# Two-phase feed-forward of the last layer: earlier residual store, another product order, snapshots ahead of SiLU, token tiles copied out of PSUM

## What is computed

```
def conv_ffn(h, w_up, conv_w, conv_b, w_down):        # h: 1024 x 1024, w_up: 1024 x 5632, w_down: 2816 x 1024
    u = h @ w_up
    up = jnp.pad(u, ((0, 0), (1, 1), (0, 0)))
    u = sum(up[:, j:j + T] * conv_w[j] for j in range(3)) + conv_b
    gate, val = jnp.split(u, 2, axis=-1)
    return (jax.nn.silu(gate) * val) @ w_down
...
f = conv_ffn(modulate(x, mod[3], mod[4]), ...)
x = layer_norm(DEEPNORM_ALPHA * x + mod[5] * f, ln2_g[l], ln2_b[l])
```

## Time and profile before

| | us |
|---|---|
| runs | 3634.85, 3628.09, 3634.22; median 3634.22 |
| profiled execution | 3634.22; its span in the trace 3632.4 |
| PE busy | 3404.0 (94%) |
| DVE, ACT, POOL busy | 1758.7 (48%), 1195.3 (33%), 1181.7 (33%) |
| fast products begin and end on PE | 3007.7 and 3345.7 |
| second group of tokens begins on PE | 3481.1 |

### The profile page before, as it was taken

How to read it: one execution, slowest core, us unless ns; L and a number is a source line. 1 busy time by engine, 2 the same in 40 slices (tenths; PEclk the granted TensorE clock), 3 DMA queues, 4 the chain that set the end, 5 groups by cost and what they waited for, 6 DMA issues and landing times. The chain is left out here.

```text
span 3632.4 us, 57974 instructions
## 1 busy us (share of the span) xinstructions
PE 3404.0 (94%) x24535; PEld 2799.2 (77%) x24535; DVE 1758.7 (48%) x2801; ACT 1195.3 (33%) x1743; POOL 1181.7 (33%) x522
## 2 busy tenths in 40 slices
PE   7999999979999999999999899999979997998998
PEld 6777778867778888888887677788867676777877
DVE  4333563066266344333346633562085785556454
ACT  4334564124332111111113333573242334444322
POOL 2221101302233333333333222102214437886432
PEclk9999999999999999999999899999989999999999
DMA  5111002262211111111111111001152122223443
GB/s 195 29 23 30 1 2 65 82 195 53 58 35 35 41 35 35 41 35 41 35 41 65 26 24 48 1 2 36 57 172 82 46 99 64 87 70 118 168 140 114
DMA packets 288117, 229.46 MB, mean 63 GB/s; under 512 B 47068, under 2 KB 257908, under 8 KB 287860
## 3 DMA queue, kind: packets, MB, share of 16 engines
q1 hardware_dynamic: 286704, 225.28, 20.1%
q10 hardware_dynamic: 1156, 0.48, 0.0%
HBM read 201.60 MB, written 24.12 MB: 62 GB/s over the span
## 5 line engine op out<-in xcount | busy, mean ns | idle before, releaser
L1333 PE MATMUL psum<-h_hi,w_split 128*128 128x512 f32 (+1 forms) x4992 | 1186.6, 367 | 22.8 <-DVEq L766 6.2
L1027 POOL TENSOR_SCALAR w_split<-w_raw 128x1024 fp32r<-128x1024 f32 x142 | 403.1, 2839 | 2059.5 <-PE psum L1333 1322.6
L1333 PEld LDWEIGHTS psum<-h_hi,w_split 128*128 128x128 f32 x4992 | 847.7, 188 | 198.0 <-issue 28.4
L1333 PE MATMUL psum<-h_lo,w_split 128*128 128x512 f32 (+1 forms) x2496 | 650.9, 364 | 0.0
L1333 PEld LDWEIGHTS psum<-h_lo,w_split 128*128 128x128 f32 x2496 | 425.3, 189 | 78.5
L2762 DVE SCALAR_TENSOR_TENSOR f_t<-psum,vec,f_t 128x1023 f32<-128x1023 f32 x194 | 170.3, 916 | 397.1 <-ACT f_t L3493 395.1
L1029 POOL TENSOR_TENSOR w_split<-w_raw,w_split 128x1024 fp32r<-128x1024 f32 x142 | 349.6, 2462 | 11.8
L3493 ACT ACTIVATE f_t<-psum,vec 128x1280 f32<-128x1280 f32 (+1 forms) x53 | 73.2, 1380 | 529.4 <-PE psum L1333 516.3
L1333 PE MATMUL psum<-f_hi,w_split 128*128 128x512 f32 (+1 forms) x1056 | 239.8, 357 | 1.5 <-DVE f_t L2762 1.5
L1333 PEld LDWEIGHTS psum<-f_hi,w_split 128*128 128x128 f32 x1056 | 176.1, 188 | 36.3 <-issue 5.7
L2620 DVE SCALAR_TENSOR_TENSOR y_chan<-psum,mods,y_chan 128x1024 f32<-128x1024 f32 (+1 forms) x176 | 146.4, 877 | 97.7 <-PE psum L1333 97.5
(11 more groups left out here) (360 smaller groups left out, 5402.7 us busy)
## 6 DMA issues: line engine op xcount, KB each, us to landing
ada_late<-in_w_ada_dram SPq DMA_DIRECT2D x32, 1024.0 KB, 7.1
w_raw<-in_w_up_dram SPq DMA_DIRECT2D x56, 512.0 KB, 3.8
w_raw<-in_w_in_dram SPq DMA_DIRECT2D x42, 512.0 KB, 3.8
w_raw<-in_w_down_dram SPq DMA_DIRECT2D x40, 512.0 KB, 3.7
up_raw<-in_w_up_dram SPq DMA_DIRECT2D x32, 512.0 KB, 5.2
f_raw<-f_mid SPq DMA_DIRECT2D x44, 256.0 KB, 3.8
l_raw<-in_w_down_dram SPq DMA_DIRECT2D x17, 512.0 KB, 3.5
ada<-in_w_ada_dram SPq DMA_DIRECT2D x4, 2048.0 KB, 16.5
```

The source lines that it names most:

```text
L1027: pool.tensor_scalar(w_hi[:, n % 2], w_raw[:, n % 2], 1.0, None, ALU.mult).then_inc(s["w_hi_done"], 1)
L1333: last = pe.matmul(columns(key, t0, t0 + tn), weight, a[:, k, t0:t0 + tn], start=(k == order[0] and j == 0), stop=(closes and k == order[- ...
```

## The change

Five things are changed, all in the last layer's feed-forward.

1. The eight residual tiles are restored during f = 1 and 2 (before: 2 and 3), and SP stores them behind tile f = 1, ahead of the weights of f = 4.
2. `differences(k)` adds high and low parts first and takes 8 DVE passes in place of 10, and its 3 low parts, as well as the 4 of `h_lo`, go from DVE to POOL. The four rounds stand one place earlier, and operands 0 to 3 of the first group are split before the last `begin`.
3. The order of products: the high-channel block of Y comes second (before: fourth), the first Z product fourth (before: second); the operand of product 1 is now a plain weight block, not a sum. The snapshots and `joined` follow that order.
4. In ACT's queue `take(i - 1, 3)` and `take(i, 0)` stand ahead of `begin` of the value half and of `silu` of the tile before, which both move from the end of the group to behind them. In the last group the split of two steps' tokens and of the first weight is moved ahead of the last convs.
5. Token tiles 0 to 3 of the down projection are copied by ACT from their banks to `y_copy` (`out_of_banks`), which frees the banks; `last_norm` reads the copy. Their normalisations and stores are spread over steps n = FT + 3, FT + 5, FT + 6.

The diff, cut:

```diff
-                    if f == 2:
+                    if f == 1:
                         for k in range(KT):
                             sp.wait_ge(s["res_ready"], KT * 2 * l + k + 1)
                             sp.dma_start(r_mid[k], y_chan[:, k, 0:LAT]).then_inc(s["r_stored"], 16)
+                    if f == 2:
                         load_up(0)
...
-                    if n == FT + 3:
-                        for i in range(4):
+                    for i, behind in enumerate((4, 5, 7, 9)):
+                        if n == FT + behind:
                             store_out(i)
...
                     pool.tensor_tensor(two, one, a11, ALU.subtract).then_inc(s["sum_done"], 1)
-                    low(1, one)
+                    low(1, a12)
                     pool.wait_ge(s["sum_done"], 4 * i + 2)
...
                     pool.tensor_tensor(two, a12, two, ALU.subtract).then_inc(s["sum_done"], 1)
-                    low(3, a12)
+                    if i == 0:
+                        for k in range(4):
+                            pool.wait_ge(s["t_split_hi"], 13 + k)
+                            pool.tensor_tensor(h_lo[:, k, HALF:LAT], t_one[:, k], h_hi[:, k, HALF:LAT].bitcast(F32), ALU.subtract)\
+                                .then_inc(s["t_ready"], 1)
+                    low(3, one)
+                    pool.wait_ge(s["op_ready"], 7 * i + 4)
+                    pool.tensor_tensor(one, a11, a21, ALU.subtract).then_inc(s["sum_done"], 1)
                     pool.wait_ge(s["sum_done"], 4 * i + 4)
                     low(4, one)
...
+            def low_differences(k):
...
+                for n, (whole, t_hi, t_lo) in enumerate(((taken[:, 1], t3_hi, t3_lo), (taken[:, 0], t2_hi, t2_lo),
+                                                         (taken[:, 2], t4_hi, t4_lo))):
+                    pool.wait_ge(s["t_split_hi"], 3 * k + n + 1)
+                    pool.tensor_tensor(t_lo[:, k], whole, t_hi[:, k].bitcast(F32), ALU.subtract).then_inc(s["t_ready"], 1)
...
-                def product(i, j, bank, x_hi, x_lo, begins=True):
+                def product(i, j, bank, x_hi, x_lo, begins=True, made=None):
                     n = 7 * i + j
                     hi, lo = up_ops[n % 4][:, 0], up_ops[n % 4][:, 1]
                     wait((s["op_ready"], n + 1))
                     for k in range(KT // 2):
+                        if made:
+                            wait((s["t_ready"], made + k + 1))
...
                     product(i, 0, x_bank(i), *tokens(low, 0))
+                    wait((s["u_done"], 3 * (i - 1) + 1) if i else freed("F", l, fast_f - 1, 0))
+                    product(i, 1, Y_BANK, *tokens(high, 0))
+                    wait((s["snap_done"], 4 * i + 1))
+                    if i == 0:
+                        wait((s["t_ready"], 12))
+                    product(i, 2, x_bank(i), t2_hi, t2_lo, begins=False)
                     if i:
                         wait((s["u_done"], 3 * (i - 1) + 3))
-                    else:
-                        wait(freed("F", l, fast_f - 1, 0))
-                        wait((s["t_ready"], 16))
-                    product(i, 1, Z_BANK, *tokens(low, 1))
-                    wait((s["snap_done"], 4 * i + 1))
-                    product(i, 2, x_bank(i), t2_hi, t2_lo, begins=False)
-                    wait((s["u_done"], 3 * (i - 1) + 1) if i else None)
-                    product(i, 3, Y_BANK, *tokens(high, 0))
+                    product(i, 3, Z_BANK, *tokens(low, 1), made=None if i else 12)
+                    wait((s["snap_done"], 4 * i + 2))
+                    product(i, 4, x_bank(i), t3_hi, t3_lo, begins=False)
                     wait((s["snap_done"], 4 * i + 3))
-                    product(i, 4, x_bank(i), t3_hi, t3_lo, begins=False)
                     product(i, 5, Z_BANK, *tokens(high, 1), begins=False)
...
                 key = ("y", i)
-                y = final(i)
+                y = y_copy[:, i] if i < 4 else final(i)
...
-                dve.wait_ge(s["y_full"], i + 1)
+                if i < 4:
+                    dve.wait_ge(s["y_freed"], i + 1)
+                else:
+                    dve.wait_ge(s["y_full"], i + 1)
...
-                for n in range(2, 2 * FT):
+                for n in range(3, 2 * FT):
                     if n == FT + 3:
-                        for i in range(3):
+                        for i in range(2):
                             last_norm(i)
-                    if n == FT + 4:
-                        last_norm(3)
+                    if n in (FT + 5, FT + 6):
+                        last_norm(n - FT - 3)
...
+                    def whole(out_, row, cols):
+                        return dve.tensor_tensor(out_, h_hi[:, row, cols].bitcast(F32), h_lo[:, row, cols].bitcast(F32), ALU.add)
+
+                    if k:
+                        dve.wait_ge(s["t_ready"], 3 * k)
+                    also(whole(three, down, then))
+                    also(whole(t_scratch[:], down, first))
+                    also(whole(two, up, then))
+                    step(whole(four, up, first))
+                    step(dve.tensor_tensor(one, three, t_scratch[:], ALU.subtract))
+                    say("t_whole", dve.tensor_tensor(three, two, three, ALU.subtract))
+                    dve.wait_ge(s["t_whole"], 3 * k + 1)
+                    say("t_whole", dve.tensor_tensor(two, two, one, ALU.subtract))
                     dve.wait_ge(s["t_whole"], 3 * k + 2)
-                    tt(four, hi[:, up, first], two, ALU.subtract)
-                    tt(four, four, lo[:, up, first], ALU.add, whole=True)
...
-                        say("t_ready", dve.tensor_tensor(t_lo[:, k], whole, t_hi[:, k].bitcast(F32), ALU.subtract))
...
-                        dve.wait_ge(s["prod_done"], 7 * i + 4)
+                        dve.wait_ge(s["prod_done"], 7 * i + 2)
...
+                    for k in range(4):
+                        residual(k)
                     conv(2, 0)
-                    for k in range(3):
+                    for k in range(4, 8):
                         residual(k)
                     conv(2, 1)
                     gated(2)
-                    for k in range(3, 6):
-                        residual(k)
+                    dve.wait_ge(s["r_stored"], 2 * 16 * KT)
+                    differences(0)
                     conv(3, 0)
-                    for k in range(6, 8):
-                        residual(k)
                     conv(3, 1)
                     gated(3)
-                    dve.wait_ge(s["r_stored"], 2 * 16 * KT)
-                    differences(0)
+                    differences(1)
                     conv(4, 0)
-                    differences(1)
+                    differences(2)
...
                     gated(4)
-                    differences(2)
-                    conv(5, 0)
                     differences(3)
-                    last_differences()
...
-                            dve.wait_ge(s["snap_done"], 4 * i + (1, 2, 3)[n])
+                            dve.wait_ge(s["snap_done"], 4 * i + (1, 3, 3)[n])
                             joined(i, n)
+                            if n == 1 and i == N_FAST - 1:
+                                low_tokens(0)
+                                low_tokens(1)
+                        if i == N_FAST - 1:
+                            gate_weights(1)
                         conv(f, 0)
...
-                    gate_weights(1)
                     conv(FT - 1, 1)
+                    gate_weights(2)
+                    low_tokens(2)
...
+            def out_of_banks(i):
+
+                act.wait_ge(s["y_full"], i + 1)
+                say("y_freed", copy(y_copy[:, i], final(i)))
...
                     if n == FT + 3:
-                        for i in range(3):
+                        for i in range(2):
+                            out_of_banks(i)
+                        for i in range(2):
                             rstd_of(("y", i))
-                    if n == FT + 4:
-                        rstd_of(("y", 3))
+                            out_of_banks(i + 2)
+                    if n in (FT + 5, FT + 6):
+                        rstd_of(("y", n - FT - 3))
...
-                    if j in (0, 3, 6):
+                    if j in (0, 1, 6):
                         act.wait_ge(s[f"raw_landed{(i + 1) % 2}"], AGAIN + 32 * (i // 2 + 1))
                         src = raw[:, j // 6, HALF * (j > 0):HALF * (j > 0) + HALF]
                     else:
-                        of_sum = {1: 0, 2: 1, 4: 2, 5: 3}[j]
-                        act.wait_ge(s["sum_done"], 4 * i + of_sum + 1)
-                        src = up_sums[:, of_sum % 2]
+                        act.wait_ge(s["sum_done"], 4 * i + {3: 1, 2: 2, 5: 3, 4: 4}[j])
+                        src = up_sums[:, 0 if j in (3, 4) else 1]
...
-                    act.wait_ge(s["prod_done"], 7 * i + (1, 2, 3, 7)[n])
+                    act.wait_ge(s["prod_done"], 7 * i + (1, 3, 4, 7)[n])
...
```

(64 more changed lines are left out.)

39 lines of the change are left out of this document (19 added, 20 removed).

## The result

The changed kernel takes 3591.62 us (median of 4 runs, 3586.22 to 3595.54) against 3631.71 (4 runs, 3628.09 to 3634.85): ratio 0.989, 95% interval 0.987 to 0.991, 40 us faster. The forecast was 3573 and the range 3560 to 3592: the sign was right, the time stands at the very end of the range, and it is the time of a rival with a chance of 0.10, POOL as the bound (3590). A third of the gain is missing, most of it in the loop, where the forecast's main step failed.

What follows compares the result with a forecast made beforehand. The prediction took PE's order of work as the bound, with its idle time and slow clock to win. Gains of 26.1 + 24 - 1.2 + 12 = 60.9 from 3634.22 gave 3573.3, stated as 3573 us; range 3560 to 3592.

Steps and rivals of the forecast that it cites:

- POOL as the bound: Product loop: POOL's delay from meeting DVE doubles, group 20.2, loop gains only 9, 3590 us; chance 0.10.
- the forecast's main step: Product loop: snapshots ahead of SiLU and a new product order cut each group from 20.78 to 19.04 us.
- The loop: The 15 product groups of the last feed-forward: 1.74 us less each, 26.1 us gained.
- so nothing is late next: Product loop: snapshots, operands, convs and POOL's 17.2 us all ready before PE wants them, so a group takes 19.04.
- The way in: From F(2,0), first tile of the changed stretch, to the second product group: 139.0 us becomes 115, 24 gained.
- 115: Forecast time from F(2,0) to the second product group: 109.1 work, 3.7 and 0.3 waits, 1.85 slow clock.
- The one wait at F(4,0): Feed-forward tile before the products: PE waits 3.7 us for a late conv, then loses 1.85 by slow clock.
- the 0.3 for group 0: First product group: 0.3 us allowed for operand 4, as late as PE itself behind POOL's h_lo passes.
- Out of the loop: Last product into the down projection: the stall moves behind the DMA, 1.2 us lost.
- Step 3: Down projection: its weight, behind 4 MB of y_back, ready at about 23.5; PE waits 6.5, then 2.6 slow clock.
- The boundary: Token groups after the old sums: ACT's copies end waits of 7.7 and 4.0 behind them, 12 us gained.
- Slower: Product loop: every POOL pass at 2.16 gives 23.8 a group, 45 us lost, 3644; chance 0.03.

Runs made afterwards that it cites:

- b2_act_only: The kernel before, with only ACT's bias pass and SiLU moved behind take 0 and the copy of operand 4: 3604.28 us, ratio 0.992.
- e4_third_sum: The changed kernel with POOL's fourth sum in its own place, made directly behind the third: 3578.65 us, ratio 0.985.
- e5_h_lo_dve: The changed kernel with the four low parts of h_lo back on DVE and, in group 0, take 0 ahead of SiLU and the last bias pass: 3587.89 us, one run.
- u_low_dve: The changed kernel with the three low parts of each round of differences back on DVE, 11 passes a round: 3590.09 us, one run.

## Why the forecast was right, and where it was not

**The loop.** The forecast stands inside its range because the range reached to 3592; for the loop, its largest term, the mechanism was wrong. The step that failed is "so nothing is late next": a loop forecast at PE's 19.04 a group runs at POOL's 20.22, and gains 8.9 in place of 26.1. It took POOL's eleven passes as a sum, 17.2 against 19.04, and looked at how early each operand was ready in the old order. The order of products was changed, and with it POOL's: between the sum `a11 - a21` and its own low part POOL had three passes before, and has none now, while ACT's copy of the sum must lie between the two. That round trip stands bare once a group, and ACT, which waits for the sum with the bias pass and SiLU queued behind, makes a second one of it. The order's text showed this: L1087 directly ahead of L1065 of the same tile. The term itself, 26.1, is what `b2_act_only` and `e4_third_sum` measured to 0.1.

Waiting for ACT is nothing new to POOL. Before, it did so three times a group, 2.9 in all, and lost nothing by it, since PE was slower still:

```profile
3158.62 1.87 POOL L1063 TENSOR_TENSOR up_op<-up_sums,up_op 128x512 fp32r<-128x512 f32 x1 [0.78 <-ACT up_op L2996]
3160.57 2.16 POOL L1079 TENSOR_TENSOR up_sums<-up_raw,up_sums 128x512 f32<-128x512 f32 x1
3163.26 1.28 POOL L1063 TENSOR_TENSOR up_op<-up_raw,up_op 128x512 fp32r<-128x512 f32 x1 [0.54 <-ACT up_op L2996]
3166.14 3.63 POOL L1063 TENSOR_TENSOR up_op<-up_sums,up_op 128x512 fp32r<-128x512 f32 x2 [1.59 <-ACT up_op L2996]
```

In `b2_act_only` these waits shrink to 0.2 when PE speeds up. That of 0.87 can't, since the copy that POOL waits for is of the sum that it has only just made, and that of 1.24 stands behind the same copy on ACT.

The 17.2 was too small as well: 258.2 was divided by 15 groups, but the stretch holds 161 passes and not 165. A full group has 17.65 before and 18.06 after. The rival that came true, POOL as the bound, was right on who sets the pace and hit the period, 20.2, by luck. It doubled the delay from meetings with DVE, 3.0 a group more. That delay rose by 0.4; the waits make 2.1, and 0.45 is the 17.2 put right.

**The way in.** Up to the first product it is right: 96.2 measured, and 115 less a group of 19.3 is 95.7. The one wait at F(4,0) was forecast at 3.7 with 1.85 of slow clock; it is 3.55, and the four half tiles behind it take 45.33 in place of 43.52, 1.8 more (the granted clock is 0.68 in the first 5.4 us of them):

```profile
2948.73 0.70 PE L1349 MATMUL psum<-h_hi,w_split 128*128 128x512 f32 x2 [3.55 <-DVE f_gate L2782]
```

What failed is the 0.3 for group 0: it took 5.0, in waits of 1.30 (take 0 behind SiLU, five copies and a bias pass), 2.16 and 0.57 (POOL's four passes of `h_lo`, 5.0 us, ahead of operand 3's low part):

```profile
3001.06 3.06 PE L1856 MATMUL psum<-t_part,up_op 128*128 128x512 f32 x12 [1.30 <-ACT taken L3002]
...
3006.27 0.50 PE L1856 MATMUL psum<-h_hi,up_op 128*128 128x512 f32 x1 [2.16 <-POOL up_op L1065]
...
3009.88 2.97 PE L1856 MATMUL psum<-t_part,up_op 128*128 128x512 f32 x12 [0.57 <-POOL up_op L1065]
```

They are 4.03. The last 1.0 is not slow clock, though the expectation of `e5_h_lo_dve` calls it that: the granted clock is 1.00 all through group 0. Each wait costs PE some 0.3 more than the idle time that its row shows, as in the loop, where 1.42 made a group 1.74 longer before and 0.86 makes it 1.18 longer now, at a clock of 1.00 both times. I had counted when `h_lo` is ready, and not what stands behind it. And of the cause given for operands 0 and 1, low parts on POOL and 8 passes on DVE in place of 13, `u_low_dve` shows that the first is not needed: 11 passes do.

**Out of the loop.** A loss of 1.2 was forecast, a gain of 1.7 measured; the sign is wrong, and the wait stands at another place. Step 3's weight was ready 22.9 behind the last product (forecast 23.5), and PE hardly waited for it (0.52), because step 2 had stood 3.18 for its own, its gate product at 3331.02 on DVE behind both last convs. The forecast gave that delay 0.7.

```profile
3336.23 1.22 PE L1903 MATMUL psum<-w_hi,f_hi 128*128 128x512 f32 x2 [3.18 <-POOL w_lo L1107]
...
3343.90 0.73 PE L1903 MATMUL psum<-h_lo,f_hi 128*128 128x512 f32 x2 [0.52 <-POOL h_lo L1107]
```

**The boundary.** 12 forecast, 12.2 measured, and 12.5 by undoing it.

**Slower.** POOL did become the bound, but with 20.22 a group it stayed far from the 23.1 at which the whole would have been slower. For the loop by itself the point is 20.78, and that is only 0.6 away.

## What to carry to other kernels

Where engines hand pieces to and fro, compare the period that you hope for with each engine's passes plus the round trips that its own order forces on it (make a piece, wait for another engine's work on it, go on); the sum of busy time alone misses them. Waits that the engine only has because it is ahead don't count. When a change reorders the consumer, look in the producer's queue how many instructions now stand between an intermediate and its use. A buffer more for one intermediate was worth 17 us in the loop here, 13 in all. And when an edit takes a wait away, look for the second one that was nearly as late: three of these experiments moved a wait to the next in line.

## What the runs showed of the hardware

With its product cut to 2 columns, DVE still spent 1.14 us on it, until POOL's pass was over (3213.98 + 2.32 = 3216.30, and 3215.18 + 1.14 = 3216.32):

```profile
3213.98 2.32 POOL L1065 TENSOR_TENSOR up_op<-up_sums,up_op 128x512 fp32r<-128x512 f32 x1 [1.24 <-ACT up_op L3004]
...
3215.18 1.14 DVE L2805 TENSOR_TENSOR f_t<-f_t 128x2 f32<-128x2 f32 x1
```

So here an instruction of DVE with two SBUF inputs lasted until POOL's had ended, whatever its own length. In the changed loop POOL's passes take 18.06 a group where they took 17.65 before, 0.4 more from such meetings, and its bare round trips 2.1. The Trainium skill, SBUF — State Buffer, "SBUF: two separate sides", states that of a VectorE instruction with two SBUF inputs and a GpSimd instruction that reads SBUF the one that starts first holds the shared ports for the whole instruction and the other is blocked; the trace agrees.
